# Experts' input rows gathered in quarter rows and transposed in 32x32 blocks by VectorE

## What is computed

```python
def moe_swiglu(h, router_w, wg, wu, wd):
    t = h.reshape(bsz * s, d)                       # 512 tokens, d = 1024
    logits = (t @ router_w).astype(jnp.float32)     # 8 experts
    top_logits, top_idx = lax.top_k(logits, TOP_K)  # TOP_K = 2
    top_w = jax.nn.softmax(top_logits, axis=-1)
    gates = jnp.einsum('tk,tke->te', top_w, jax.nn.one_hot(top_idx, N_EXPERTS, dtype=jnp.float32))
    y = jnp.zeros_like(t)
    for e in range(N_EXPERTS):
        y = y + gates[:, e:e + 1] * ((jax.nn.silu(t @ wg[e]) * (t @ wu[e])) @ wd[e])
```

## Time and profile before

| | us |
|---|---|
| three runs | 1929.24, 1935.07, 1937.03 |
| their median | 1935.07 |
| the profiled execution | 1934.42 |
| its span, first to last instruction | 1932.5 |
| TensorE busy in it | 1893.2 |
| VectorE, ScalarE, GpSimd busy | 912.4, 578.6, 727.9 |

### The profile page before, as it was taken

The page is one execution under the profiler, slowest core; times in us unless marked ns, Lnnn a source line. Parts: engine busy times, 40 slices in busy tenths (PEclk is TensorE's granted clock), DMA queues, the critical chain, the costliest instruction groups (busy, mean ns, idle before and its releaser), DMA issues. The chain is left out here.

```text
span 1932.5 us, 36862 instructions
## 1 busy us (share of the span) xinstructions
PE 1893.2 (98%) x15078; PEld 1629.3 (84%) x15078; DVE 912.4 (47%) x1225; ACT 578.6 (30%) x1234; POOL 727.9 (38%) x624
## 2 busy tenths in 40 slices
PE   9999999999999999999999999999999999999997
PEld 8778745888887888888877887778999999999996
DVE  3898687677565455444436777765100000000023
ACT  1443213455533111110036657543120211111102
POOL 5755522565544434444526777651300000000011
PEclk9999999999999999999999999999999999999999
DMA  9213750222215666631212111201957578778893
GB/s 332 91 55 142 266 206 25 81 98 88 83 44 198 212 205 214 217 121 60 103 66 67 67 56 61 74 13 70 322 207 248 197 233 276 256 262 334 336 348 155
DMA packets 82824, 313.58 MB, mean 162 GB/s; under 512 B 10121, under 2 KB 10641, under 8 KB 82529
## 3 DMA queue, kind: packets, MB, share of 16 engines
q1 hardware_dynamic: 75952, 289.73, 42.5%
q0 software_dynamic: 4464, 14.35, 2.1%
q10 hardware_dynamic: 2241, 7.14, 1.0%
HBM read 301.43 MB, written 9.75 MB: 161 GB/s over the span
## 5 line engine op out<-in xcount | busy, mean ns | idle before, releaser
L261 PE MATMUL banks<-sb_act,sb_ring 128*64 128x112 f32 (+9 forms) x5088 | 620.9, 300 | 1.2 <-ACT sb_ring L468 0.7
L261 PEld LDWEIGHTS banks<-sb_act,sb_ring 128*128 128x128 f32 (+1 forms) x5088 | 592.4, 174 | 23.2 <-issue 4.5
L261 PE MATMUL banks<-sb_x_norm,sb_ring 128*128 128x256 f32 (+3 forms) x1616 | 330.9, 403 | 3.4 <-ACT sb_ring L468 2.3
L261 PEld LDWEIGHTS banks<-sb_x_norm,sb_ring 128*128 128x128 f32 (+1 forms) x1616 | 242.4, 171 | 66.3 <-issue 29.6
L3730 DVE TENSOR_TENSOR sb_act<-sb_work,banks 128x192 f32<-128x192 f32 (+7 forms) x88 | 27.2, 309 | 482.7 <-PE banks L261 475.4
L443 POOL TENSOR_TENSOR sb_ring<-sb_ring 128x512 f32<-128x512 f32 x146 | 206.7, 1415 | 104.2 <-PE banks L261 53.7
L261 PE MATMUL banks<-sb_work,sb_ring 128*64 128x256 f32 (+2 forms) x1124 | 231.6, 407 | 3.2 <-ACT sb_ring L468 2.1
L261 PEld LDWEIGHTS banks<-sb_work,sb_ring 128*128 128x128 f32 (+1 forms) x1124 | 155.9, 165 | 56.9 <-issue 34.6
L3261 POOL DMA_INDIRECT sb_work<-first_expert_rows,sb_table x8 | 7.5, 939 | 442.9 <-DMA first_expert_rows<-sb_x_norm 440.8
L3532 ACT ACTIVATE sb_work<-banks 128x192 f32<-128x192 f32 (+7 forms) x88 | 25.8, 294 | 295.2 <-PE banks L261 293.2
L2370 ACT ACTIVATE sb_work<-banks 128x256 f32<-128x256 f32 x84 | 32.3, 384 | 216.8 <-PE banks L261 216.8
(11 more groups left out here) (530 smaller groups left out, 2589.2 us busy)
## 6 DMA issues: line engine op xcount, KB each, us to landing
sb_ring<-in_w_moe_up SPq DMA_DIRECT2D x176, 512.0 KB, 4.7
sb_ring<-in_w_moe_down SPq DMA_DIRECT2D x64, 704.0 KB, 6.5
sb_act<-in_cond_w SPq DMA_DIRECT2D x84, 512.0 KB, 3.7
sb_ring<-in_w_ffn_up SPq DMA_DIRECT2D x44, 512.0 KB, 5.1
sb_ring<-in_w_h_in SPq DMA_DIRECT2D x32, 512.0 KB, 4.3
sb_ring<-in_w_in SPq DMA_DIRECT2D x28, 512.0 KB, 6.2
sb_ring<-in_w_m_in SPq DMA_DIRECT2D x24, 512.0 KB, 4.0
sb_ring<-in_w_ffn_down SPq DMA_DIRECT2D x16, 704.0 KB, 5.4
```

The source lines that it names most:

```text
L261: last = m.nc.tensor.matmul(out[part], weights[:, part], act, start=start, stop=stop, skip_group_check=skip)
```

## The change

The token rows are stored as quarter rows: `d_rows` becomes 2048 x 256. GpSimd first copies each group of `x_rows` with its 32-element pieces in another order, so that quarter q holds, for each of the eight 128-feature tiles, features 32q to 32q + 31, and then stores it; ScalarE stores nothing. The list of tokens now holds 4 times the token number and is loaded four times, once into each group of 32 partitions, with q added in group q. A tile takes four indirect DMAs of 128 quarter rows each; partition group q gets quarter q of 32 tokens. VectorE then turns a tile with four transposes of 32x32 blocks straight into `xT`, and ScalarE scales `xT` in place. TensorE's `turn` is gone, with PSUM banks 4 to 7 free of it.

The core of the diff:

```diff
@@ -148,7 +148,8 @@
         self.mod = sb("mod", [P, 96])
         self.cond = sb("cond", [P, KD])
         self.small = sb("small", [P, 64])
-        self.table = sb("table", [P, 3 * ST + GATHERS + 1 + EXPERTS + 4 * ST], U32)
+        self.table = sb("table", [P, 3 * ST + 1 + EXPERTS + 4 * ST], U32)
+        self.row_parts = sb("row_parts", [P, 4 * GATHERS], U32)
         self.rank_caps = sb("rank_caps", [P, EXPERTS])
         self.rank_first = sb("rank_first", [P, EXPERTS])
         self.rank_at = sb("rank_at", [P, EXPERTS])
@@ -157,7 +158,7 @@
         self.spare = sb("spare", [P, 2, S])
         dram = lambda n, shape, dt=F32: nc.dram_tensor(n, shape, dt, kind="Internal").ap()
         self.d_tokens = dram("tokens_of_expert", (PASSES * ROWS, 1), U32)
-        self.d_rows = dram("normed_rows", (S, D))
+        self.d_rows = dram("normed_rows", (4 * S, DG))
         self.d_first = dram("first_expert_rows", (FIRST[-1] + ROWS - sum(CAPS), D))
         self.d_result = dram("expert_rows", ((PASSES - 1) * ROWS, D))
         self.d_gate_rows = dram("gate_rows", (2 * HEADS, S))
@@ -3129,10 +3130,13 @@
     used = [len(range(s, total, SLOTS)) for s in range(SLOTS)]
     uses = list(m.stream.uses)
     per_pass = EXPERTS * total
-    over_at = 3 * ST + GATHERS
+    over_at = 3 * ST
     too_many = m.table[0:1, over_at:over_at + 1]
-    token_rows = m.table[:, 3 * ST:3 * ST + GATHERS]
-    tokens = m.d_tokens.rearrange("(p t q) o -> p q (t o)", t=GATHERS, q=P)
+    tokens = m.d_tokens.rearrange("(p g q) o -> p q (g o)", g=4 * GATHERS, q=QUARTER)
+    by_quarter = lambda t: t.rearrange("p (q k c) -> p k q c", q=4, c=QUARTER)
+    stored_rows = m.d_rows.rearrange("(t q) c -> t (q c)", q=4)
+    quartered = [t.rearrange("p a c -> p (a c)") for t in (m.HN[:, 0:2, :], m.HN[:, 2:4, :], m.HN[:, 4:6, :], m.more[:])]
+    row_parted = m.sem("r_row_parted")
     order = m.sem("e_order")
     BUFS = 8
     x0_banks = (6, 7, 0, 1, 2, 3)
@@ -3222,6 +3226,11 @@
                     nc.gpsimd.indirect_dma_start(
                         m.d_tokens, bass.IndirectOffsetOnAxis(ap=m.table[:, j * ST + t:j * ST + t + 1], axis=0),
                         m.table[:, 2 * ST + t:2 * ST + t + 1], None).then_inc(scattered, 16)
+            for t in range(ST):
+                pool.wait_ge(row_out, t + 1)
+                give(pool, nc.gpsimd.tensor_copy(by_quarter(quartered[t]), x_rows[:, t, :].rearrange(
+                    "p (k q c) -> p k q c", q=4, c=QUARTER)), row_parted, t + 1)
+                pool.dma_start(stored_rows[rows(t, P), :], quartered[t]).then_inc(row_stored, 16)
             pool.wait_ge(scattered, 16 * 2 * ST)
             pool.wait_ge(row_stored, 16 * ST)
             pool.wait_ge(x0_made, KD)
@@ -3232,17 +3241,24 @@
                     for i in range(2):
                         pool.wait_ge(y_stored[i], stored_by(i, p))
                     pool.sem_inc(order, 1)
-                pool.dma_start(token_rows, tokens[p], allow_slow_non_contiguous=True).then_inc(idx_in, 16)
-                pool.wait_ge(idx_in, p * 16 + 16)
+                for q in range(4):
+                    pool.dma_start(m.row_parts[rows(q, QUARTER), :], tokens[p],
+                                   allow_slow_non_contiguous=True).then_inc(idx_in, 16)
+                pool.wait_ge(idx_in, p * 64 + 64)
                 pool.sem_inc(order, 1)
+                for q in range(1, 4):
+                    part = m.row_parts[rows(q, QUARTER), :]
+                    m.glink.on(pool)(nc.gpsimd.tensor_scalar(part, part, q, None, ALU.add))
                 for i in range(first_pass(p), GATHERS):
                     if i > BUFS or not first_pass(p) and i == BUFS:
                         pool.wait_ge(turned, p * GATHERS + (i - BUFS))
                         pool.sem_inc(order, 1)
-                    nc.gpsimd.indirect_dma_start(
-                        got[i % BUFS], None, m.d_rows,
-                        bass.IndirectOffsetOnAxis(ap=token_rows[:, i:i + 1], axis=0)
-                    ).then_inc(got_sem[i % BUFS], 16)
+                    for q in range(4):
+                        c = 4 * i + q
+                        nc.gpsimd.indirect_dma_start(
+                            got[i % BUFS][:, rows(q, DG)], None, m.d_rows,
+                            bass.IndirectOffsetOnAxis(ap=m.row_parts[:, c:c + 1], axis=0)
+                        ).then_inc(got_sem[i % BUFS], 16)
                 if not first_pass(p):
                     return
                 pool.wait_ge(turned, GATHERS - 1)
@@ -3339,19 +3355,8 @@
 
             def body(p):
 
-                def turn(i):
-                    pe.wait_ge(got_sem[i % BUFS], p * (16 * got_used[i % BUFS]) + 16 * (
-                        i // BUFS + (i % BUFS > 0) + (not first_pass(p))))
-                    if not first_pass(p) or i >= 3:
-                        pe.wait_ge(turned_out, p * GATHERS + (i - 2))
-                    for k in range(KD):
-                        last = nc.tensor.transpose(ps[:, 4 + 2 * (i % 2) + k // 4, rows(k % 4, P)],
-                                                   got[i % BUFS][:, rows(k, P)], m.c("ident"))
-                    last.then_inc(turned, 1)
-
                 def turn_result(r):
                     pe.wait_ge(m.evac, p * per_pass + (r * total + done + total))
-                    pe.wait_ge(turned_out, p * GATHERS + (need[min(r + 1, EXPERTS - 1)] - 1))
                     for k in range(KD):
                         last = nc.tensor.transpose(ps[:, 4 + k // 4, rows(k % 4, P)], yT[:, k, 0:P], m.c("ident"))
                     width = tail_at[r] + CAPS[r] - P
@@ -3363,8 +3368,6 @@
                 if not first_pass(p):
                     pe.wait_ge(y_copied, p * copies)
                     pe.sem_inc(order, 1)
-                    for i in range(need[0]):
-                        turn(i)
                 for r in range(EXPERTS):
                     base, cap = r * total + done, CAPS[r]
                     m.strip = 64 if cap < P else P
@@ -3384,8 +3387,6 @@
                             if 0 < r <= turned_ranks:
                                 pe.wait_ge(y_copied, p * copies + copies_until(r - 1))
                                 pe.sem_inc(order, 1)
-                            for i in tiles_beside(p, r):
-                                turn(i)
                             pe.wait_ge(m.evac, p * per_pass + (base + up))
                             pe.sem_inc(order, 1)
                         pe.wait_ge(m.loaded[s], p * (16 * used[s] * EXPERTS) + 16 * (uses[s] + r * used[s] + b // SLOTS + 1))
@@ -3471,7 +3472,6 @@
                 give(act, nc.scalar.activation(x_rows[:, t, :].rearrange("p (a c) -> p a c", c=S),
                                                ps[:, 2 * (t % 2):2 * (t % 2) + 2, :], ACT.Copy,
                                                scale=norm.inv[:, t:t + 1]), row_out, t + 1)
-                act.dma_start(m.d_rows[rows(t, P), :], x_rows[:, t, :]).then_inc(row_stored, 16)
             for k in range(KD):
                 act.wait_ge(x0_made, k + 1)
                 nc.scalar.activation(xT[:, k, 0:CAP], ps[:, x0_banks[k % len(x0_banks)], 0:CAP], ACT.Identity,
@@ -3482,10 +3482,9 @@
             def body(p):
                 def take_turned(i):
                     act.wait_ge(turned, p * GATHERS + i)
-                    pair = 4 + 2 * (i % 2)
                     for k in range(KD):
-                        last = nc.scalar.activation(xT[:, k, rows(i, P)], ps[:, pair + k // 4, rows(k % 4, P)],
-                                                    ACT.Identity, bias=norm.shift(k), scale=norm.scale(k))
+                        x = xT[:, k, rows(i, P)]
+                        last = nc.scalar.activation(x, x, ACT.Identity, bias=norm.shift(k), scale=norm.scale(k))
                     last.then_inc(turned_out, 1)
 
                 def take_result(r):
@@ -3533,6 +3532,8 @@
                                              ACT.Silu).then_inc(silu, 1)
                     for i in tiles_beside(p, r):
                         take_turned(i)
+                    if first_pass(p) and r == 0:
+                        act.wait_ge(row_stored, 16 * ST)
                     if closing:
                         nc.scalar.preload_act_table_set("natural_log_exp_and_others")
                     for d in range(down - closing):
@@ -3652,7 +3653,7 @@
             step(nc.vector.tensor_reduce(most, cap_of, AX, ALU.max))
             step(nc.vector.tensor_scalar(most, most, 0.0, None, ALU.max))
             step(nc.vector.tensor_copy(m.table[:, over_at:over_at + 1], most))
-            step(nc.vector.tensor_copy(m.table[:, 2 * ST:3 * ST], m.c("tok_id")))
+            step(nc.vector.tensor_scalar(m.table[:, 2 * ST:3 * ST], m.c("tok_id"), 4.0, None, ALU.mult))
             give(dve, nc.vector.tensor_copy(m.table[:, 0:2 * ST], m.small[:, 3 * ST:5 * ST]), tables, 1)
             dve.wait_ge(exp_out, 1)
             step(nc.vector.tensor_scalar(w1, w2, 1.0, None, ALU.add))
...
```

(15 more changed lines are left out.)

## The result

The changed kernel takes 1938.18 us (median of 20 runs, 1935.33 to 1941.57), the kernel before in the same comparison 1933.33 us (20 runs, 1929.24 to 1937.03). The ratio is 1.0025, 95% interval [1.0019, 1.0031]: 4.85 us longer, half of the 0.5% that the chances count as a difference, but clearly on the other side of 1 than the forecast, which had taken 1.96 us off the one profiled execution of 1934.42 us. The profiled execution of the changed kernel has a span of 1938.1 us, the one before 1932.5.

A forecast was written before the change was run, and what follows sets the result against it. The prediction took TensorE, busy for 98% of the span, as the bound. A gain of 1.96 us and costs of 0 elsewhere turned the profiled 1934.42 us into 1932.5, range 1928.5 to 1942.0.

The forecast's parts named there:

- part 4: GpSimd's copies, stores, index loads, additions and gathers until rank 0 needs tile 2: hidden with slack 7.0 us, cost 0.
- Part 1: 72 transposes leave TensorE ahead of the down products: gain 1.96 us, the other 6.7 us become waiting.
- The rival that the whole 8.64 comes back: Ahead of the down products, all of TensorE's transpose time is gained: 1925.8 us; chance 0.05.
- Part 2: VectorE turns tiles behind a rank's last product, 0.45 us a transpose, then ScalarE scales them: hidden, cost 0.
- The rival of slow transposes: VectorE's transposes take 1.7 us each, delaying TensorE at ranks 1 to 6: about 1938 us; chance 0.04.
- Part 3: ScalarE stops storing normed rows; neither TensorE's first gather products nor the later stores beside weight loads change the time: 0.
- the library instruction: One more GpSimd library instruction ahead of its first addition: between 0 and 14.8 us, taken as 7.
- GpSimd late: Index loads queue, TensorE stands at rank 0's fifth down block: 1942.7 us, 1950.5 with the library's upper bound; chance 0.19.
- The clock rival: Seven new TensorE pauses of about 0.9 us lower the clock, costing 21 us: 1953; chance 0.04.

The follow-up runs named there:

- e1: The changed kernel with one more wait: GpSimd's four row copies wait for VectorE's last-rank slot tiles; 1932.44 us, ratio 0.9996.
- e2: The kernel before, plus only GpSimd's four reordering copies behind the scatters, results unused; 1937.55 us, ratio 1.0021.
- e7: e1 plus 4 idle TensorE products ahead of the wait for VectorE's last product at ranks 0 to 5; 1932.51 us, ratio 0.9994.
- e4: The changed kernel with 36 idle TensorE products ahead of rank 0's fifth up block; 1939.62 us, ratio 1.0035.
- e6: e1 with TensorE's turning of the previous rank's results moved into the pause ahead of the down products, ranks 1 to 5; 1927.2 us, ratio 0.9966.
- e5: The changed kernel with 18 idle TensorE products ahead of rank 0's fifth up block; 1936.15 us, ratio 1.0014.

## Why the prediction was wrong

**The failed step is part 4, GpSimd's four row copies.** The prediction priced them on GpSimd's own line (1.90 us each) and followed the chain to the point where tile 2 is wanted. It named no engine that works beside the copies. They end long before anything needs them, and it called them free. What they touch is VectorE, between 1361 and 1368.5, where the same instructions end 4.4 us later than before, at a point at which VectorE had no slack. The row that would have shown it was in the trace of before and not read: VectorE's first product of rank 0 starts at 1364.19, right behind the routing. The page's 47% for VectorE says nothing of the one moment at which it is the bound. What the runs show in place of a cost of 0 is 4.46 us of standing and 2.52 us of lower clock. e1 shows that the copies' place alone decides this; e2 shows that copies without anything else of the change cost 4.75 us.

The Trainium skill has the rule (SBUF — State Buffer, Who interferes with whom): VectorE's second pair of SBUF ports is GpSimd's only one, a lock held for a whole instruction, and a VectorE instruction with two SBUF inputs or in a 2-port mode blocks while GpSimd has it. The trace agrees in both directions: two-input and TENSOR_SCALAR instructions stand until the 1.04 us copy has ended, and products with one operand in PSUM keep their 0.35 us beside it. In which mode the TENSOR_SCALAR instructions ran, and so whether this rule covers them, no run shows; the two-input ones it covers. The prediction cited another page and left this one out, though it would have changed the sum.

**Part 1 was right.** VectorE's end plus 0.27 sets the start of the down products: 1418.79 + 0.35 = 1419.14, start at 1419.42, 0.28 later, as the timeline of after has it:

```profile
1418.79 0.35 DVE L3742 TENSOR_TENSOR sb_act<-sb_work,banks 128x192 f32<-128x192 f32 x1 [4.84 <-PE banks L262]
...
1419.07 2.72 DVE L3729 STREAM_TRANSPOSE sb_act<-sb_work 128x256 f32<-128x256 f32 x8
1419.42 6.63 PEld L262 LDWEIGHTS banks<-sb_act,sb_ring 128*128 128x128 f32 x41 [1.06 <-issue]
...
1420.52 5.88 ACT L3487 ACTIVATE sb_act<-sb_act,sb_mod 128x128 f32<-128x128 f32 x15 [4.09 <-DVE sb_act L3729]
```

The seven pauses are 1.06, 1.03, 0.96, 0.94, 0.90, 0.90 and 0.92 us, 6.71 in sum, where 6.7 was forecast. The gain of 1.96 us is in e1's stage, 1.97 without the difference in weight waits. The rival that the whole 8.64 comes back is refuted, and e7 shows why: work put back into the pauses moves nothing.

**Part 2 was right.** The 36 transposes take 409 ns each in the mean (0.45 taken), eight in 2.72 us, and no down block waits for ScalarE. ScalarE's 16 activations in place take 6.26 us, 0.39 each where 0.36 was kept. The rival of slow transposes falls; that it named about 1938 us, the time then measured, is chance.

**Part 3 was right**: TensorE's first gather products ran without a pause, 64 loads in 10.38 us before and after. In rank 7 TensorE waits 1.12 us for weights after the change, 1.24 in e1 and 0.68 in e4, against 0.91 before; no run explains these differences.

**Part 4's chain was faster than taken**, and its slack held. The last store is issued at 1368.64 (1373.3 taken). It lands 9.5 us later where 6 was taken, so the index loads begin at 1378.77, hardly earlier than the forecast 1379.3. The four index loads, then the additions and the first gather:

```profile
1378.77 3.44 POOL L3245 DMA_DIRECT2D sb_row_parts<-tokens_of_expert  x4 [9.60 <-issue]
1388.42 1.10 POOL L3251 TENSOR_SCALAR sb_row_parts<-sb_row_parts 32x40 uint32<-32x40 uint32 x3 [6.21 <-DMA sb_row_parts<-tokens_of_expert]
1389.81 1.10 POOL L3258 DMA_INDIRECT sb_work<-normed_rows,sb_row_parts  x1 [0.28 <-POOL sb_row_parts L3251]
```

A copy is 1.04 us, near the lower end of 0.99 and not the 1.90 taken. The loads overlap, landing 6.21 us after the last issue, and no rest is left for the library instruction: its 7 us were 0, or hidden under that load. The first gather is at 1389.8, 9 us ahead of the forecast 1399, and 7 of the 9 are the library's term. So the slower side that the prediction did have, GpSimd late, is refuted as well; that its range (up to 1942.0) holds 1938.18 is owed to that rival and not to the real cause.

**The clock rival was right that a pause can cost clock, and wrong in place and size.** It asked whether pauses of 0.9 us lower the clock; none did, at any of seven places. The clock fell behind a pause that the prediction didn't know, by 2.5 us.

What stays open: the four held VectorE instructions are on record as started up to 0.5 us before the copy that held them (1361.09 against 1361.57). By their usual 0.29 to 0.35 us three of them would have ended before it. Records of GpSimd's spans are rough, and no run settles when the hold begins, nor whether the end of the DMA issue ahead of a copy already belongs to it.

## What to carry to other kernels

Before an elementwise instruction is put on GpSimd, look at what VectorE does in the same microseconds, and how much slack it has at that place; for each GpSimd copy, one VectorE instruction that reads SBUF alone is to be counted longer, here by 0.66 to 1.40 us. One wait that puts the copies behind VectorE's last such instruction was worth some 5.7 us here (1938.18 to 1932.44; ratios to before 1.0025 and 0.9996), and 6.85 us in the stage. When an engine's work is replaced by waiting, look for its own later work that can be done in the wait: the transposes' removal gave nothing measurable in the whole time (e1), the 0.9 us that it opened at each rank gave 5.2 us once results were turned there (e1's 1932.44 to e6's 1927.2; 4.22 of them in the stage).

## What the hardware showed that was not expected

- A VectorE instruction that reads SBUF only stands until a GpSimd copy ends: 1.01 to 1.69 us in place of 0.29 to 0.35, one instruction for each copy. One with an operand in PSUM doesn't stand at all (0.35).
- Behind pauses of TensorE of 4.46 and 3.29 us the granted clock went from 1.00 to 0.50 for some microseconds, and the 288 loads that followed took 2.52 and 1.67 us longer; behind 1.91 us and behind all pauses of about 0.9 it stayed at 1.00. Idle products in the pause kept it at 1.00 (e4, e5).
- A GpSimd copy of 128x1024 fp32 in pieces of 32 took 1.04 us, and a VectorE transpose of 128x256 fp32 in 32x32 blocks 0.34 us from start to start, written with a stride. An idle fp32 product is two weight loads (18 products, 36 loads in 4.15 us), a transpose against the identity one.
